# Expert stage of a two-layer decoder step: tokens split once, dispatch in float32r, the gate applied in the accumulate, the combine over five banks

## The chip, the cores and the metric

The program runs on one core of one Trainium2 chip. The metric is the device time of one execution in microseconds (us); lower is better. The engines are TensorE (PE in the rows; PEld is its weight load), VectorE (DVE), ScalarE (ACT), GpSimd (POOL) and SyncE (SP), which issues the loads of weights.

## The reference, cut to what matters

Two layers of a hybrid decoder are computed for 256 prompt tokens and 8 sample tokens, in float32. The change is in the last stage, the mixture of experts: each token goes to its two best experts of eight, with gates from a softmax over the two logits.

```
def moe_swiglu(h, router_w, wg, wu, wd):
    logits = (h @ router_w).astype(jnp.float32)
    top_v, top_i = lax.top_k(logits, TOP_K)
    gates = jax.nn.softmax(top_v, axis=-1)
    comb = jnp.sum(jax.nn.one_hot(top_i, N_EXPERTS, dtype=jnp.float32) * gates[..., None], axis=-2)
    out = jnp.zeros_like(h)
    for e in range(N_EXPERTS):
        out = out + comb[..., e:e + 1].astype(h.dtype) * swiglu(h, wg[e], wu[e], wd[e])
    return out
```

The model width is 1024 and an expert is 3584 wide, so an expert has three matrices of 1024 x 3584 (44.04 MB in float32).

## The kernel before, in words

Large products are made in three passes of float32r: each operand is split into a high part (ScalarE copies it to a float32r tile) and a low part (VectorE subtracts the high part from the original), and TensorE adds lo x hi, hi x lo and hi x hi in one PSUM bank. Weights come as pieces of 1 MB (128 partitions x 2048 floats). SyncE loads them into seven raw places (six in `weight_ring`, one in `work`); `take_hi` (L467 is its copy) and `take_lo` (L470 its subtraction) write the halves into three places of `weight_hi` and `weight_lo`. The dense layers in front do the same by L762 to L764.

An expert takes 42 pieces: seven steps c = 0..6, each with a gate product g, an up product u (both by `product`, L2009 to L2011: two pieces, 24 matmuls of 512 columns) and, one step late, a down product (`down`, L2024). Products go to banks 0 to 3 (g into bank 0 or 2, u into 1 or 3), transposes of the activation to bank 4 (L1993), the expert's output to banks 5 and 6.

Around the weights, per expert:

- `select` (DVE, L1534 and L1535) writes two matrices of one row per token and one column per slot (128 slots): `sel` with ones where the token's rank is the slot, and `selw` with the token's gate in that place. It runs for the next expert in step c = 2, behind the activation product L1557 and in front of the next L470.
- `dispatch` (PE, L1983) gathers the expert's tokens: `h_tok` (264 tokens in three tiles of 128, 128 and 8, float32) times `sel`, 24 matmuls of 128 columns into banks 7 and 3. It runs in front of the last `down`. L1048 (ACT) and L1542 (DVE) split the result into `hte_h` and `hte_l`, the second waiting for the first.
- Behind the g product of step 0 of the next expert comes `combine` (PE, L2040 and L2041) for the expert that is done: six tiles (two halves of 512 columns by three token tiles), two matmuls each, into the three banks 7, 3, 2 in turn. From the fourth tile on PE waits for `add_up` (DVE, L1584) to have emptied the bank of three tiles before. `add_up` stands in DVE's order behind `take_lo` of the fourth piece.
- Then PE transposes `sel` into bank 4 (L2058, three) and multiplies `selw` with a column of ones (L2060, three), which gives the gate of each slot. ACT copies that column to `slot_gate` (L1076) and the transposes to `ST` (L1077); `slot_gate` scales the output when it is split into `y_hi` (L1070) and `y_lo` (L1571).

The order within each engine is the program's; there is no scheduler. ACT and DVE follow PE through the counts `piece_used`, `hi_done` and `lo_done`. Before the first expert PE transposes x and h to token rows (L1962, 24 each through banks 0 to 3), ACT copies them (L1042), and masks and ranks are made in between (L1479 to L1522, L1968, L1972).

Of the kernel before, what the change touches and what calls it, by code (L numbers as in the profile page):

```python
# [14 lines left out]
P = 128  # L15
# [8 lines left out]
def program(nc, A, O):  # L24
# [31 lines left out]
    with ExitStack() as ctx:  # L56
# [30 lines left out]
        def order(engine, *events):  # L87
            first = 0
            for name, count in events:
# [11 lines left out]
              ("xtok", 6), ("htok", 6))  # L101
# [8 lines left out]
              ("iota_psum", 1), ("logits_psum", 1), ("xtok_psum", 6), ("htok_psum", 6), ("ranks_psum", 1))  # L110
# [7 lines left out]
              ("out_o_added", KD), ("norm3_inv", 1), ("norm3_done", 1), ("iota", 1), ("top_diff", 1), ("masks", 1), ("ranks", 1))  # L118


# [35 lines left out]
        W = 17696  # L156
        work = sb("work", [P, W])
# [248 lines left out]
        h_tok = cut(QKV0, NTT, D)  # L406
        raw_last = cut(QKV0 + NTT * D, PIECE)
        mo = [QKV0 + NTT * D + PIECE]

        def more_of(*dims):  # L410
            v = cut(mo[0], *dims)
            mo[0] += math.prod(dims)
            assert mo[0] <= W
            return v

        sel = more_of(NTT, CAP)
        selw = more_of(NTT, CAP)
        slot_gate = more_of(1)
# [13 lines left out]
        FAR = 16384.0  # L432

# [350 lines left out]
        def _(act_e):  # L784
# [253 lines left out]
            for s, dst in (("xtok", acc), ("htok", h_tok)):  # L1038
                for i, (t0, n) in enumerate(TOK):
                    for k in range(YC):  # L1040
                        act_e.wait_ge(*at(s + "_psum", i * YC + k + 1))
                        SC.activation(dst[0:n, i, k * CHUNK_COLS:(k + 1) * CHUNK_COLS],  # L1042
                                      bank[(i * YC + k) % 4][0:n, :], ACT.Copy).then_inc(sig(s), 1)

            def dispatch_out(it, r):
                act_e.wait_ge(*at("moe_disp", it * 2 + r + 1))
                n = KD // 2
                SC.activation(hte_h[:, r * n:(r + 1) * n, :], bank[(7, 3)[r]][:, :].rearrange("p (j t) -> p j t", j=n), ACT.Copy)\  # L1048
                  .then_inc(sig("hte_hi"), 1)
# [5 lines left out]
            def act_expert(it, more):  # L1055
                for n, (kind, c, part) in enumerate(order_e):
# [10 lines left out]
                    if n == PER - 1:  # L1067
                        wait_used(act_e, it, "d", NSTEP - 1)
                        for hf in range(YC):
                            SC.activation(y_hi[:, hf * CHUNK_COLS:(hf + 1) * CHUNK_COLS], bank[5 + hf][:, :], ACT.Copy,  # L1070
                                          scale=slot_gate).then_inc(sig("y_high"), 1)
# [24 lines left out]
        def _(dve):  # L1096
# [380 lines left out]
            norm_dve(dve, 3, "ln_ffn_o", link)  # L1477
            dve.wait_ge(*at("iota_psum", 1))
# [34 lines left out]
            last.then_inc(sig("masks"), 1)  # L1513
            dve.wait_ge(*at("ranks_psum", 1))
# [16 lines left out]
            def select(e):  # L1531

                for i, (t0, n) in enumerate(TOK):
                    V.tensor_scalar(sel[0:n, i, :], iota[0:n, 0:CAP], column(rank, i, n, e), None, ALU.is_equal)  # L1534
                    last = V.tensor_scalar(selw[0:n, i, :], iota[0:n, 0:CAP], column(rank, i, n, e), column(comb, i, n, e),  # L1535
                                           ALU.is_equal, ALU.mult)
                last.then_inc(sig("sel"), 1)

            def hte_lo(it, r):
                dve.wait_ge(*at("hte_hi", it * 2 + r + 1))  # L1540
                n = KD // 2
                V.tensor_tensor(hte_l[:, r * n:(r + 1) * n, :], bank[(7, 3)[r]][:, :].rearrange("p (j t) -> p j t", j=n),  # L1542
                                hte_h[:, r * n:(r + 1) * n, :].bitcast(F32), ALU.subtract).then_inc(sig("hte"), 1)
# [6 lines left out]
            def dve_expert(it, owed, more, e_next):  # L1550
                for n, (kind, c, part) in enumerate(order_e):
                    if kind == "g" and part and c:
                        tr_lo(it, c - 1)
                    if kind == "u" and part:
# [3 lines left out]
                        if c == 2 and more:  # L1558
                            dve.wait_ge(*at("moe_w", it + 1))
                            select(e_next)  # L1560
# [5 lines left out]
                    if n == PER - 1:  # L1566
                        wait_used(dve, it, "d", NSTEP - 1)
                        for hf in range(YC):
                            cols = slice(hf * CHUNK_COLS, (hf + 1) * CHUNK_COLS)
                            dve.wait_ge(*at("y_high", it * YC + hf + 1))  # L1570
                            V.scalar_tensor_tensor(y_lo[:, cols], bank[5 + hf][:, :], slot_gate, y_hi[:, cols].bitcast(F32),  # L1571
                                                   ALU.mult, ALU.subtract).then_inc(sig("y_out"), 1)
                    if n == 1 and owed:
                        add_up(it - 1)
# [3 lines left out]
            def add_up(it):  # L1578
                for k in range(NTT * YC):
# [4 lines left out]
                    V.tensor_tensor(a, a, bank[(7, 3, 2)[k % 3]][0:n, :], ALU.add).then_inc(sig("added"), 1)  # L1584
# [5 lines left out]
            dve_expert(0, False, True, 1)  # L1590
            with dve.Fori(1, NE - 1) as e:
                dve_expert(e, True, True, e + 1)
# [540 lines left out]
```

## Time and profile before

| what | value |
|---|---|
| median of 3 runs | 2059.72 us (2058.79 to 2063.31) |
| profiled execution, first to last instruction | 2062.8 us |
| PE busy | 1855.5 us, 90% of the span |
| DVE busy | 1366.5 us, 66% |
| ACT busy | 1041.4 us, 50% |
| mean granted clock of TensorE | 0.904 |
| expert stage | from about 955 us to the end |

The profile gives no other time of its execution than the span; it is 3.1 us above the median of the runs. "Busy" of PE counts pipelined matmuls as long as they last, so distances between starts say more than durations: a 512-column float32r matmul lasts 0.39 us and the next starts 0.23 us later.

### The profile page before, as it was taken

Reading aid. Unit: us, or ns where it says so; the run is one execution under the profiler, and the core shown is the slowest. Engines: PE = TensorE matmul, PEld = TensorE weight load, DVE = VectorE, ACT = ScalarE, POOL = GpSimd, SP = SyncE. Lnnn points to the kernel's source line nnn. Section 1 sums busy time; section 2 is a strip of 40 time slices with the busy share of each in tenths; the row PEclk is TensorE's granted clock in tenths of the full one; section 3 lists DMA queues with packets and bytes.
Section 4 is the critical chain, followed back from the end, with each engine's and each line's share of the span. In section 5 each row is a group of like instructions: output and inputs, shape, how many; then the busy total and the mean of one; then the engine's idle time right before and its main releaser. Section 6 shows DMA issues by size and latency. Waiting matters only on the chain.

```text
span 2062.8 us, 25677 instructions
## 1 busy us (share of the span) xinstructions
PE 1855.5 (90%) x9920; PEld 1566.0 (76%) x9920; DVE 1366.5 (66%) x1599; ACT 1041.4 (50%) x964; POOL 41.0 (2%) x92
## 2 busy tenths in 40 slices
PE   4967789998988678878999999999999999999997
PEld 4935689898976666476887887878878878788786
DVE  3564334444776555542887878878868788688786
ACT  3442233333652211022776766757757667577574
POOL 1011000000001000000000000000000000000000
PEclk9975789997998887575999999999999999999999
DMA  6443125442450002420897988988969889789794
GB/s 194 146 160 85 70 94 178 160 165 97 164 175 16 1 1 62 112 88 15 314 378 266 363 329 290 369 285 325 373 244 365 319 301 365 282 319 370 278 368 153
DMA packets 199084, 445.51 MB, mean 216 GB/s; under 512 B 9457, under 2 KB 20883, under 8 KB 198959
## 3 DMA queue, kind: packets, MB, share of 16 engines
q1 hardware_dynamic: 182206, 423.75, 57.1%
q0 software_dynamic: 3872, 12.85, 2.2%
q10 hardware_dynamic: 12924, 7.77, 1.3%
q8 instruction: 57, 0.93, 0.2%
q14 instruction: 25, 0.20, 0.0%
HBM read 437.28 MB, written 7.29 MB: 216 GB/s over the span
## 4 chain that ended last, share of the span: by engine, by line
PE 75%; DVE 11%; ACT 6%; issue 3%; PEld 2%; DMA 1%; ACTq 1%; PEldq 0%; DVEq 0%; POOLq 0%; POOL 0%
PE bank L2024 13%; PE bank L2009 10%; PE bank L2010 9%; PE bank L2011 9%; PE bank L762 5%; PE bank L763 5%; PE bank L764 4%; PE bank L1983 4%; ACT weight_hi L467 2%; DVE weight_lo L470 2%; PE bank L707 1%; PE bank L1861 1%; PE bank L1993 1%; PE bank L1856 1%; DVE work L1320 1%
## 5 line engine op out<-in xcount | busy, mean ns | idle before, releaser
L470 DVE TENSOR_TENSOR weight_lo<-weight_ring,weight_hi 128x2048 fp32r<-128x2048 f32 (+1 forms) x358 | 810.2, 2272 | 356.6 <-ACT weight_hi L467 356.5
L467 ACT ACTIVATE weight_hi<-weight_ring 128x2048 fp32r<-128x2048 f32 (+1 forms) x358 | 681.0, 1904 | 370.1 <-PE bank L764 152.3
L2009 PE MATMUL bank<-weight_hi,h_lo 128*128 128x512 f32 x896 | 360.4, 402 | 3.8 <-DVE weight_lo L470 2.3
L2010 PE MATMUL bank<-weight_lo,h_hi 128*128 128x512 f32 x896 | 353.7, 395 | 0.0
L2011 PE MATMUL bank<-weight_hi,h_hi 128*128 128x512 f32 x896 | 353.5, 395 | 0.0
L762 PE MATMUL bank<-h_hi,weight_lo 128*128 128x264 f32 x1072 | 313.7, 293 | 26.1 <-DVE h_lo L742 14.2
L763 PE MATMUL bank<-h_lo,weight_hi 128*128 128x264 f32 x1072 | 311.0, 290 | 0.0
L764 PE MATMUL bank<-h_hi,weight_hi 128*128 128x264 f32 x1072 | 309.0, 288 | 0.0
L762 PEld LDWEIGHTS bank<-h_hi,weight_lo 128*128 128x128 f32 x1072 | 208.2, 194 | 32.4 <-DVE h_lo L742 15.8
L763 PEld LDWEIGHTS bank<-h_lo,weight_hi 128*128 128x128 f32 x1072 | 208.2, 194 | 0.0
L764 PEld LDWEIGHTS bank<-h_hi,weight_hi 128*128 128x128 f32 x1072 | 207.6, 194 | 0.0
L2009 PEld LDWEIGHTS bank<-weight_hi,h_lo 128*128 128x128 f32 x896 | 171.4, 191 | 41.1 <-DVE weight_lo L470 4.5
L2011 PEld LDWEIGHTS bank<-weight_hi,h_hi 128*128 128x128 f32 x896 | 171.0, 191 | 36.9
L2010 PEld LDWEIGHTS bank<-weight_lo,h_hi 128*128 128x128 f32 x896 | 171.5, 191 | 34.2
L2024 PE MATMUL bank<-weight_hi,h_lo 128*128 128x512 f32 x448 | 139.3, 392 | 1.8 <-DVE h_lo L1547 1.8
L2024 PE MATMUL bank<-weight_lo,h_hi 128*128 128x512 f32 x448 | 138.8, 391 | 0.0
L2024 PE MATMUL bank<-weight_hi,h_hi 128*128 128x512 f32 x448 | 138.5, 390 | 0.0
L470 DVE TENSOR_TENSOR weight_lo<-work,weight_hi 128x2048 fp32r<-128x2048 f32 x48 | 109.9, 2290 | 12.7 <-ACT weight_hi L467 12.7
L467 ACT ACTIVATE weight_hi<-work 128x2048 fp32r<-128x2048 f32 x48 | 92.2, 1921 | 28.4 <-PE bank L2011 22.0
L2024 PEld LDWEIGHTS bank<-weight_hi,h_lo 128*128 128x128 f32 x448 | 83.8, 188 | 19.9 <-DVE h_lo L1547 2.1
L2024 PEld LDWEIGHTS bank<-weight_hi,h_hi 128*128 128x128 f32 x448 | 84.6, 189 | 17.8
L2024 PEld LDWEIGHTS bank<-weight_lo,h_hi 128*128 128x128 f32 x448 | 84.5, 189 | 17.6
(422 smaller groups left out, 1828.9 us busy)
## 6 DMA issues: line engine op xcount, KB each, us to landing
weight_ring<-in_moe_wg SPq DMA_DIRECT2D x104, 1024.0 KB, 6.8
weight_ring<-in_moe_wu SPq DMA_DIRECT2D x96, 1024.0 KB, 7.3
weight_ring<-in_moe_wd SPq DMA_DIRECT2D x88, 1024.0 KB, 6.2
work<-in_moe_wd SPq DMA_DIRECT2D x24, 1024.0 KB, 7.1
weight_ring<-in_w_in_o SPq DMA_DIRECT2D x8, 2048.0 KB, 8.5
work<-in_moe_wu SPq DMA_DIRECT2D x16, 1024.0 KB, 5.2
weight_ring<-in_w_in_e SPq DMA_DIRECT2D x5, 2048.0 KB, 14.0
weight_ring<-in_ffn_wg SPq DMA_DIRECT2D x5, 2048.0 KB, 7.9
```

Of the source, the lines that this page charges most:

```text
L467: return SC.activation(whi[:, p % SPLIT, 0:size], src, ACT.Copy).then_inc(sig("hi_done"), 1)
L470: V.tensor_tensor(wlo[:, p % SPLIT, 0:size], src, whi[:, p % SPLIT, 0:size].bitcast(F32), ALU.subtract)\
L707: last = PE.matmul(bank[4][0:m, i:i + 1], inv[:, j, t0:t0 + m], ones[:, 0:1], start=j == 0, stop=j == KD - 1)
L762: PE.matmul(out, lo[:, jj, cols_], h_hi[:, j0 + j, :], start=first and j == 0, stop=False)
L763: PE.matmul(out, hi[:, jj, cols_], h_lo[:, j0 + j, :], start=False, stop=False)
L764: last = PE.matmul(out, hi[:, jj, cols_], h_hi[:, j0 + j, :], start=False, stop=last_one and j == k - 1)
L1320: V.scalar_tensor_tensor(o[:, back:TP], x[:, 0:TP - back], tap(m, j), o[:, back:TP], ALU.mult, ALU.add)
L1983: last = PE.matmul(bank[(7, 3)[r]][:, jj * CAP:(jj + 1) * CAP], h_tok[0:n, i, j * P:(j + 1) * P], sel[0:n, i, :], start=i == 0, stop=i == ...
L2009: PE.matmul(out, hte_l[:, j, :], hi[:, jj, :], start=j == 0, stop=False)
L2010: PE.matmul(out, hte_h[:, j, :], lo[:, jj, :], start=False, stop=False)
L2011: last = PE.matmul(out, hte_h[:, j, :], hi[:, jj, :], start=False, stop=j == KD - 1)
L2024: last = PE.matmul(bank[5 + hf][:, :], lhs[:, c % 2, k, :], rhs[:, kk, hf * CHUNK_COLS:(hf + 1) * CHUNK_COLS], start=c == 0 and k == 0 and ...
```

## The change

- `h_tok` is split once into `tok_hi` and `tok_lo` (float32r, by the new ACT copy and DVE subtraction through six banks). The third token tile is padded with zeros to 128 rows, for which DVE writes three memsets.
- `dispatch` multiplies both parts with `sel`, which is float32r now, into a bank each: 48 matmuls in place of 24, and always 128 rows deep. ACT copies the high bank and DVE the low bank; neither waits for the other.
- `selw`, the products with the column of ones, `slot_gate` and its copy are gone. `add_up` multiplies by the token's gate as it adds.
- `combine` goes over five banks: 7, 3, 2, 5, 6. PE waits for `add_up` from the sixth tile on.
- Before the first expert, h is transposed first, then ranks, then x. `work` is placed first in SBUF, so that float32r tiles can lie over it.

```
-            for s, dst in (("xtok", acc), ("htok", h_tok)):
+            act_e.wait_ge(*at("tok_clear", 2))
+            for s, dst, banks in (("htok", tok_hi, TOK_BANKS), ("xtok", acc, X_BANKS)):
...
-            SC.activation(y_hi[...], bank[5 + hf][:, :], ACT.Copy, scale=slot_gate).then_inc(sig("y_high"), 1)
+            SC.activation(y_hi[...], bank[5 + hf][:, :], ACT.Copy).then_inc(sig("y_high"), 1)
...
-                        SC.activation(slot_gate, bank[4][:, T:T + 1], ACT.Copy)
...
+            V.memset(tok_hi[:, TT, :].bitcast(F32), 0.0).then_inc(sig("tok_clear"), 1)
+            V.memset(tok_lo[:, TT, :].bitcast(F32), 0.0).then_inc(sig("tok_clear"), 1)
+            V.memset(sel[:].bitcast(F32), 0.0).then_inc(sig("tok_clear"), 1)
...
+                    dve.wait_ge(*at("htok", i * YC + k + 1))
+                    V.tensor_tensor(tok_lo[0:n, i, part], bank[TOK_BANKS[i * YC + k]][0:n, :], tok_hi[0:n, i, part].bitcast(F32), ALU.subtract)\
+                     .then_inc(sig("htok_lo"), 1)
...
-                    V.tensor_scalar(sel[0:n, i, :], iota[0:n, 0:CAP], column(rank, i, n, e), None, ALU.is_equal)
-                    last = V.tensor_scalar(selw[0:n, i, :], iota[0:n, 0:CAP], column(rank, i, n, e), column(comb, i, n, e),
-                                           ALU.is_equal, ALU.mult)
+                    last = V.tensor_scalar(sel[0:n, i, :], iota[0:n, 0:CAP], column(rank, i, n, e), None, ALU.is_equal)
...
             def hte_lo(it, r):
-                dve.wait_ge(*at("hte_hi", it * 2 + r + 1))
+                dve.wait_ge(*at("moe_disp", it * 2 + r + 1))
...
-                    V.tensor_tensor(a, a, bank[(7, 3, 2)[k % 3]][0:n, :], ALU.add).then_inc(sig("added"), 1)
+                    V.scalar_tensor_tensor(a, bank[COMBINE_BANKS[k % 5]][0:n, :], column(comb, i, n, e), a, ALU.mult, ALU.add)\
+                     .then_inc(sig("added"), 1)
...
-                        last = PE.matmul(bank[(7, 3)[r]][:, jj * CAP:(jj + 1) * CAP], h_tok[0:n, i, j * P:(j + 1) * P],
-                                         sel[0:n, i, :], start=i == 0, stop=i == NTT - 1)
+                for part, src in enumerate((tok_hi, tok_lo)):
+                    for jj in range(KD // 2):
+                        j = r * (KD // 2) + jj
+                        for i in range(NTT):
+                            last = PE.matmul(bank[DISPATCH_BANKS[r][part]][:, jj * CAP:(jj + 1) * CAP], src[:, i, j * P:(j + 1) * P],
+                                             sel[:, i, :], start=i == 0, stop=i == NTT - 1)
...
-                    if k >= 3:
-                        pe.wait_ge(*at("added", (it + 1) * (NTT * YC) + (k - 2)))
+                    if k >= 5:
+                        pe.wait_ge(*at("added", (it + 1) * (NTT * YC) + (k - 4)))
...
-                        for i, (t0, n) in enumerate(TOK):
-                            last = PE.matmul(bank[4][:, T:T + 1], selw[0:n, i, :], ones[0:n, 0:1], start=i == 0, stop=i == NTT - 1)
```

## Rows read from the trace of the kernel before

**Rows 1.** The page: busy us (share of the span) and instructions of each engine.

```profile
PE 1855.5 (90%) x9920; PEld 1566.0 (76%) x9920; DVE 1366.5 (66%) x1599; ACT 1041.4 (50%) x964; POOL 41.0 (2%) x92
```

**Rows 2.** The page: the chain that ended last, by engine.

```profile
PE 75%; DVE 11%; ACT 6%; issue 3%; PEld 2%; DMA 1%; ACTq 1%; PEldq 0%; DVEq 0%; POOLq 0%; POOL 0%
```

**Rows 3.** The chain in order of time, end of one expert: start, us, what.

```profile
1223.70 0.44 PE bank L1993 x4
1224.14 8.24 PE bank L1983 x48
1232.38 5.68 PE bank L2024 x24
```

**Rows 4.** Timeline of PE, a dense layer: starts, durations, line and shape.

```profile
520.85 0.28 PE L764 MATMUL bank<-h_hi,weight_hi 128*128 128x264 f32 x1
...
522.05 0.29 PE L762 MATMUL bank<-h_hi,weight_lo 128*128 128x264 f32 x1
```

**Rows 5.** Timeline of PE, first dispatch; granted clock (PEclk) behind the busy times.

```profile
956.57 15.03 PE L1983 MATMUL bank<-work 128*128 128x128 f32 x48 [2.96 <-DVE work L1535]
973.01 0.79 PE L2009 MATMUL bank<-weight_hi,h_lo 128*128 128x512 f32 x1 [1.41 <-DVE h_lo L1542]
...
957.00:971.50 14.50, 14.50 (x48) 10.94 (x47) 0.69 (x1) 0.60 (x1) 0.00 (x0) 0.50 0.01 1
```

**Rows 6.** Timeline between two experts at 1238 us: DVE and ACT.

```profile
1239.53 1.40 DVE L1571 SCALAR_TENSOR_TENSOR h_lo<-bank,work,h_hi 128x512 fp32r<-128x512 f32 x2
...
1244.42 2.29 DVE L470 TENSOR_TENSOR weight_lo<-weight_ring,weight_hi 128x2048 fp32r<-128x2048 f32 x1 [0.94 <-ACT weight_hi L467]
1246.63 3.65 DVE L1584 TENSOR_TENSOR work<-work,bank 128x512 f32<-128x512 f32 x6
...
1241.18 1.28 ACT L467 ACT_TABLE_LOAD   x1
```

**Rows 7.** Timeline of PE, the combine between two experts at 1110 us.

```profile
1110.67 0.39 PE L2041 MATMUL bank<-h_hi,sel_slots 128*8 128x512 f32 x1
1113.58 0.50 PE L2040 MATMUL bank<-h_lo,sel_slots 128*128 128x512 f32 x1 [2.52 <-DVE work L1584]
...
1115.24 0.54 PE L2058 MATMUL bank<-ident,work 128*128 128x128 f32 x3
...
1116.55 0.50 PE L2009 MATMUL bank<-weight_hi,h_lo 128*128 128x512 f32 x1
```

**Rows 8.** Timeline in step c = 2: DVE, then PE.

```profile
1289.31 0.28 DVE L1534 TENSOR_SCALAR work<-work 128x128 f32<-128x128 f32 x1
...
1290.67 4.47 DVE L470 TENSOR_TENSOR weight_lo<-weight_ring,weight_hi 128x2048 fp32r<-128x2048 f32 x2
...
1293.00 0.50 PE L2009 MATMUL bank<-weight_hi,h_lo 128*128 128x512 f32 x1 [0.33 <-DVE weight_lo L470]
```

**Rows 9.** Windows over two boundaries: PE, PEld, DVE, ACT, POOL busy, clock, DMA share, GB/s.

```profile
1108.00:1122.00 14.00, 11.48 (x53) 8.44 (x52) 10.20 (x10) 8.65 (x8) 0.00 (x0) 1.00 0.75 256
1244.80:1258.80 14.00, 11.48 (x40) 8.64 (x40) 8.14 (x9) 5.66 (x6) 0.00 (x0) 0.76 0.65 224
```

**Rows 10.** Timeline of DVE: starts of the output's split, later experts.

```profile
1105.74 1.40 DVE L1571 SCALAR_TENSOR_TENSOR h_lo<-bank,work,h_hi 128x512 fp32r<-128x512 f32 x2
...
1376.32 1.40 DVE L1571 SCALAR_TENSOR_TENSOR h_lo<-bank,work,h_hi 128x512 fp32r<-128x512 f32 x2
...
1924.88 0.75 DVE L1571 SCALAR_TENSOR_TENSOR h_lo<-bank,work,h_hi 128x512 fp32r<-128x512 f32 x1
```

**Rows 11.** Timeline of PE: the other long waits of the stage.

```profile
1931.78 0.47 PE L2040 MATMUL bank<-h_lo,sel_slots 128*128 128x512 f32 x1 [1.58 <-DVE work L1584]
...
2043.44 0.72 PE L2024 MATMUL bank<-weight_hi,h_lo 128*128 128x512 f32 x2 [1.84 <-DVE h_lo L1547]
...
2052.42 0.50 PE L2040 MATMUL bank<-h_lo,sel_slots 128*128 128x512 f32 x1 [1.63 <-DVE h_lo L1571]
```

**Rows 12.** DMA from 1150 to 1838 us: rate in 40 slices.

```profile
GB/s 341 365 380 368 280 244 242 366 336 361 390 370 252 246 246 366 356 367 375 372 233 249 248 374 355 366 383 379 208 262 254 375 342 374 382 368 208 275 219 375
```

More of the change, by code:

```diff
@@ L117, in program, with over @@
               ("l2_applied", 2 * HC), ("s_prod", 1), ("on_inv", 1), ("on_applied", HC), ("on_done", 2), ("on_lo", 2),
-              ("out_o_added", KD), ("norm3_inv", 1), ("norm3_done", 1), ("iota", 1), ("top_diff", 1), ("masks", 1), ("ranks", 1))
+              ("out_o_added", KD), ("norm3_inv", 1), ("norm3_done", 1), ("iota", 1), ("top_diff", 1), ("masks", 1), ("htok_lo", 6), ("ranks", 1))
+        W = 17696
+        WORK_AT = -(-nc.sbuf_base // 32) * 32
+        work = sb("work", [P, W])
+        assert nc.sbuf_base == WORK_AT + 4 * W
+        def over(name, at_, shape, dt):
+            assert at_ + math.prod(shape[1:]) <= W
+            return nc.alloc_sbuf_tensor_at(name, shape, dt, offset=WORK_AT + 4 * at_)
         ring = sb("weight_ring", [P, SLOTS, KD * CHUNK_COLS])
@@ L1559, in dve_expert @@
                             dve.wait_ge(*at("moe_w", it + 1))
-                            select(e_next)
+                            select(e + 1)
                     if n == PER - 3:
@@ L1952, in _ @@
             last.then_inc(sig("logits_psum"), 1)
-            for s, src in (("xtok", xT), ("htok", hT)):
-                for i, (t0, n) in enumerate(TOK):
-                    for k in range(YC):
-                        r = i * YC + k
-                        if r >= 4:
-                            pe.wait_ge(*at(s, r - 3))
-                        elif s == "htok":
-                            pe.wait_ge(*at("xtok", NTT * YC))
-                        for m in range(KF):
-                            last = PE.transpose(bank[r % 4][0:n, m * P:(m + 1) * P], src[:, k * KF + m, t0:t0 + n], ident[:])
-                        last.then_inc(sig(s + "_psum"), 1)
+            pe.wait_ge(*at("iota", 1))
+            for i, (t0, n) in enumerate(TOK):
+                for k in range(YC):
+                    for m in range(KF):
+                        last = PE.transpose(bank[TOK_BANKS[i * YC + k]][0:n, m * P:(m + 1) * P], hT[:, k * KF + m, t0:t0 + n], ident[:])
+                    last.then_inc(sig("htok_psum"), 1)
             pe.wait_ge(*at("masks", 1))
@@ L1973, in _ @@
             last.then_inc(sig("ranks_psum"), 1)
-            pe.wait_ge(*at("htok", NTT * YC))
+            for i, (t0, n) in enumerate(TOK):
+                for k in range(YC):
+                    r = i * YC + k
+                    if r < 4:
+                        pe.wait_ge(*at("htok_lo", r + 1))
+                    else:
+                        pe.wait_ge(*at("xtok", r - 3))
+                    for m in range(KF):
+                        last = PE.transpose(bank[X_BANKS[r]][0:n, m * P:(m + 1) * P], xT[:, k * KF + m, t0:t0 + n], ident[:])
+                    last.then_inc(sig("xtok_psum"), 1)
+            pe.wait_ge(*at("htok_lo", NTT * YC))
+            pe.wait_ge(*at("xtok", NTT * YC))
             pe.wait_ge(*at("flag", 1))
@@ L2057, in pe_expert @@
                         for i, (t0, n) in enumerate(TOK):
-                            PE.transpose(bank[4][:, t0:t0 + n], sel[0:n, i, :], ident[0:n, 0:n])
-                        for i, (t0, n) in enumerate(TOK):
-                            last = PE.matmul(bank[4][:, T:T + 1], selw[0:n, i, :], ones[0:n, 0:1], start=i == 0, stop=i == NTT - 1)
+                            last = PE.transpose(bank[4][:, t0:t0 + n], sel[0:n, i, :].bitcast(F32), ident[0:n, 0:n])
                         last.then_inc(sig("moe_w"), 1)
```

64 lines of the change are left out of this document (33 added, 31 removed).

## The prediction

> **What bounds the kernel now.** I read the page first: TensorE is busy 90% of the span, VectorE 66%, ScalarE 50% [rows 1]. Then the chain of waits: PE carries 75% of it, DVE 11%, ACT 6% [rows 2]. So what PE does in the expert stage is on the path, and what DVE and ACT do is on it only where PE stands still. The chain in order of time shows the change's first piece: at the end of an expert the dispatch takes 8.24 us between the transposes and the last down product, and the down product runs on behind it without a gap [rows 3]. Last I read the timeline between two experts. PE runs the next g product and three combine tiles, then idles 2.52 us for the first `add_up` and does the rest [rows 7]; `add_up` starts at 1246.63, as soon as DVE is through the piece begun at 1244.42, which itself waited for ACT (a table load stands there) [rows 6]. In step c = 2 PE idles 0.33 us more, behind DVE [rows 8].
>
> I make the sum against the profiled execution, 2062.8 us from first to last instruction, and take off the 3.1 us by which it stands over the median of 2059.72.
>
> **The dispatch.** Before: 24 float32 matmuls, 48 records, 8.24 us [rows 3], so 0.172 us a record and 0.343 a matmul. After: 48 float32r matmuls of 128 moving columns. No float32r matmul under 264 columns is in the trace, so this price is unknown. From below: a float32 transpose, one record with 128 columns each way, costs 0.44 / 4 = 0.11 us [rows 3]. The float32r matmul of 264 columns costs (522.05 - 520.85) / 10 = 0.12 [rows 4]; a shorter one should not cost more. From above: the same as the float32 matmul of this shape, 0.343. I take 0.114, between the two single-record rows, since a float32r matmul is one record everywhere in this trace: 48 x 0.114 = 5.5 us, or 2.7 us less. Seven dispatches in the loop: 7 x 2.74 = 19.2 us (17 to 21 by the two near rows, a loss of 7 x 8.3 = 58 by the far one). The padded third tile costs nothing by itself: tiles of 8 rows already count in the 48 records like full ones. Behind the dispatch ACT's and DVE's copies start from its end as before, and so does ACT's first new piece; it all shifts with PE.
>
> The Trainium skill would price it lower (TensorE: Matmul & The Clock Gate, Back-to-back issue gap): a sustained stream of weight load and matmul at 128 columns takes about 81 ns a matmul. By that the dispatch would be an estimated 3.9 us and the loop's gain 30 us. The trace's one-record transposes, at 110 ns, don't run that fast, so I leave it out of the sum.
>
> The eighth, in front of the first expert, ran its 15.03 us at a granted clock of 0.50, the 1.2 GHz level [rows 5]. At twice 5.5 it takes 11.0: 4.0 us less. Behind it PE waited 1.41 us for ACT's copy and then DVE's [rows 5]; now they run side by side, which takes the shorter of the two, some 0.6 us, off. Its start I leave where it is. `select` has half the instructions (0.7 us less) and PE's h transposes no longer wait behind x. But DVE has six subtractions of 512 columns, 0.6 to 0.7 us each, between masks and ranks, and PE's x transposes end later. The three memsets lie under the router product, when DVE idles. Together 4.6 us, between 1 and 7.
>
> **The combine and the gate products.** DVE's order up to `add_up` is unchanged, so PE still waits for its first addition to end. Before, at the full clock, 2.97 us passed from then to the first matmul of the u product (1113.58 to 1116.55) [rows 7]: tiles four to six, three transposes, three products with the column of ones. After, only tile six is left, about 0.48 us, and the transposes, 0.46 (1115.24 to 1115.70): 0.95. So 2.0 us at each of seven boundaries, 14.1. Expert 0, which has no combine, loses its three gate products, 0.85. Together 15.0. Tiles four and five run earlier, in time in which PE idled, and the idle shrinks from 2.52 to about 1.6 us.
>
> What is late next: the fifth piece. `add_up` with a scalar per token costs what L1571 costs, 0.70 us apart [rows 6], where L1584 took 0.61; six of them end 0.5 us later, and PE comes to that piece 2 us earlier. By the rows it is ready some 0.6 us before PE needs it. If that cover is gone it costs up to 0.5 us a boundary, 3.5 in all. The last `add_up`, behind the last expert, is exposed: 0.1 to 0.5 us, within the rest.
>
> **The selection in step 2.** Six instructions in 1.36 us (1289.31 to 1290.67), then two pieces, then PE starts late [rows 8]. Three are left, 0.7 us less. PE's idle there is 0.33 us by the row; starts are about 0.7 us late against the usual 0.23 us distance. I take 0.65 x 7 = 4.6 us (2.3 if the row's idle is all).
>
> **The clock.** At one boundary of two shown the granted clock stays 1.00 over 14 us, at the other it is 0.76 [rows 9]; of the other four that the loop runs through, each falls too, and the one in front of the last expert doesn't. The price: from 1105.74 to 1239.53 are 133.8 us, from 1239.53 to 1376.32 (with 1239.53 in [rows 6]) 136.8 [rows 6, 10]. So a fall costs 3.0 us. From 1105.74 to 1924.88 six experts take 819.1 us [rows 10]; six times 133.8 is 802.7, so the five falls cost 16.4 (one is longer than the others). Which idle brings a fall? 2.52 us brought one at five of six boundaries. Of the other three long waits of the stage, 1.58 and 1.63 us brought none and 1.84 brought one [rows 11]. The idle of 1.6 us after the change lies with the first two, but it is followed by small work. I take two falls out of seven boundaries: 10.4 us gained (16.4 with none, a loss of 5 with seven).
>
> **The sum:** 19.2 + 4.6 + 15.0 + 4.6 + 10.4 = 53.8 us. 2062.8 - 53.8 = 2009.0 in the profile, 2006 as a median.
>
> **Rivals.**
>
> *A short float32r matmul is no cheaper than a float32 one* (the other side). At 0.343 us each, the dispatch takes 16.5 us: 11 more than in my sum, seven times, and 22 more in the first: 99 us, so 2105. For it: no row of the trace shows float32r at 128 columns, and float32 at that shape costs three times a transpose. Against: at 264 and 512 columns float32r costs one record a matmul. It decides from about 0.24 us a matmul on, where the dispatch's loss eats the other 30 us. The Trainium skill speaks against it (FP8 and Floating Point Precision): true float32 is four passes through the array. By it 48 single passes replace 96.
>
> *A short float32r matmul costs in between*, from the 0.172 us of a float32 record to 0.22. The dispatch is then 8.3 to 10.6 us; 25 to 46 us of the sum go: 2031 to 2052.
>
> *The clock goes on falling.* Everything else as forecast, but five to seven falls: 9 to 15 us more, 2015 to 2021. For it: the fall at 1.84 us is near, and after the wait come a tile of 8 tokens and transposes. Against: the fall-free waits of 1.58 and 1.63.
>
> *The loads become the bound.* An expert would have about 128 us for its 44.04 MB, 345 GB/s, and between boundaries already takes 366 to 384 [rows 12]. So the pace inside an expert is one the loads hold now, and no wait of ACT's copies for a load is seen. Only the pauses shrink, where the rate sinks to 210 to 280. If the loads could hold just 340 GB/s on average, it would cost some 2 us an expert: 2022.
>
> **Chances.** My forecast (dispatch at 0.08 to 0.14 us a matmul, up to four falls) 0.60; clock falling on 0.14; in between 0.15; loads 0.04; no cheaper 0.07. Less than 0.2%, 4 us, can't be told from no change by runs like these. All but the last rival end below 2055: faster 0.91; slower 0.07, and 0.02 for a price that hits the break-even. The likeliest case by itself spans 1990 (no fall, 0.08 us a matmul) to 2017. The range reaches to the in-between case's middle: 1990 to 2042.
>
> **What would show it.** L1983's successor: 48 records in about 5.5 us behind the transposes; 8 or more is a rival. PE's wait for `add_up` at 1.6 us, before the last tile alone. The u product 0.95 us after it. No idle before the g product of step 3. Granted clock near 1.00 at most boundaries. From one L1571 to the next about 128 to 129 us where the clock holds. The prediction is wrong if the short float32r matmuls are not single records, or if the earlier PE meets a piece of weights that is not yet split.

## The result, and the profile after

| kernel | median, us | lowest to highest | profiled span |
|---|---|---|---|
| before, in the same session | 2059.26 | 2057.53 to 2063.31 | 2062.8 |
| changed | 1990.7 | 1985.54 to 1993.12 | 1988.1 |

The ratio is 0.9657, 95% interval 0.9641 to 0.9672: 3.4% faster. On the 2059.72 us that the forecast started from this is 1989.1 us. The forecast was 2006, with a range from 1990 to 2042: the direction is right, and the gain of 70.6 us is larger than the 53.8 of the forecast, and just past the end of its range. The same kernel run again in a later session gave 1985.47 us (1984.19 to 1989.14), ratio 0.9641 (0.9623 to 0.966), so two sessions of one kernel lie up to 5 us apart.

The page of the changed kernel, busy times and the chain by engine. PE loses 59 us of busy time against [rows 1], and its share of the chain rises from 75% [rows 2] to 78%: less of the path is now time in which PE stands still.

```profile
PE 1796.3 (90%) x9872; PEld 1533.9 (77%) x9872; DVE 1368.7 (69%) x1584; ACT 1039.4 (52%) x956; POOL 41.0 (2%) x92
...
PE 78%; DVE 10%; ACT 4%; issue 2%; PEld 2%; DMA 1%; ACTq 1%; PEldq 0%; POOLq 0%; DVEq 0%; POOL 0%
```

The chain in order of time, at the end of one expert (start, us, what). This answers [rows 3]: the dispatch takes 5.31 us where it took 8.24.

```profile
1201.40 0.44 PE bank L2019 x4
1201.84 5.31 PE bank L2009 x48
1207.15 5.54 PE bank L2050 x24
```

The timeline of PE at the first dispatch, and two windows over it (us, busy of PE, PEld, DVE, ACT, POOL, granted clock, DMA share, GB/s). It answers [rows 5].

```profile
949.90 1.53 PE L2009 MATMUL bank<-sel,tok_hi 128*128 128x128 f32 x12 [0.72 <-issue]
...
955.29 2.76 PE L2009 MATMUL bank<-sel,tok_lo 128*128 128x128 f32 x12
958.88 0.76 PE L2035 MATMUL bank<-weight_hi,h_lo 128*128 128x512 f32 x1 [0.83 <-ACT h_hi L1060]
...
949.90:952.50 2.60, 2.60 (x23) 2.60 (x24) 0.00 (x0) 0.00 (x0) 0.00 (x0) 0.99 0.02 6
952.50:958.10 5.60, 5.55 (x27) 5.36 (x26) 0.70 (x2) 0.61 (x2) 0.00 (x0) 0.50 0.00 0
```

The 15.03 us have become 8.1 (949.90 to 958.05). The first half of the matmuls now runs at a granted clock of 0.99 (the 2.4 GHz level), the rest at 0.50 (1.2 GHz). In front PE waits 0.72 us, not 2.96, and behind 0.83, not 1.41.

The timeline of PE and DVE between two experts, answering [rows 7]. One combine tile, the last, is left behind the wait. From its start to the first u product 0.93 us pass.

```profile
1091.97 0.39 PE L2067 MATMUL bank<-h_hi,sel_slots 128*128 128x512 f32 x1
1093.05 4.02 DVE L1602 SCALAR_TENSOR_TENSOR work<-bank,work 128x512 f32<-128x512 f32 x6
1093.85 0.39 PE L2066 MATMUL bank<-h_lo,sel_slots 128*8 128x512 f32 x1 [1.50 <-DVE work L1602]
...
1094.32 0.54 PE L2085 MATMUL bank<-ident,sel 128*128 128x128 f32 x3
1094.78 0.50 PE L2035 MATMUL bank<-weight_hi,h_lo 128*128 128x512 f32 x1
```

Windows over two boundaries, same columns, answering [rows 9]. The granted clock is 1.00 at both, and so it is at the other five.

```profile
1086.00:1100.00 14.00, 12.51 (x57) 9.56 (x56) 12.35 (x13) 10.78 (x8) 0.00 (x0) 1.00 0.81 291
1214.00:1228.00 14.00, 12.51 (x57) 9.57 (x56) 12.36 (x13) 10.81 (x8) 0.00 (x0) 1.00 0.79 290
```

The timeline of DVE, start of the output's split, answering [rows 10]. From the first to the second row is one expert, 128.0 us; from the first to the third are six, 768.3 us, 128.05 each.

```profile
1086.14 1.28 DVE L1589 TENSOR_TENSOR h_lo<-bank,h_hi 128x512 fp32r<-128x512 f32 x2
...
1214.17 1.28 DVE L1589 TENSOR_TENSOR h_lo<-bank,h_hi 128x512 fp32r<-128x512 f32 x2
...
1854.45 1.28 DVE L1589 TENSOR_TENSOR h_lo<-bank,h_hi 128x512 fp32r<-128x512 f32 x2
```

From these marks, profile against profile, the 74.7 us divide so:

| stretch | forecast | measured |
|---|---|---|
| up to the router product (935.73 before, 930.01 after) | 0 | 5.7 |
| h/x transposes to the first split of an output (162.76, now 148.88) | 8.8 | 13.9 |
| six experts (819.14, now 768.31) | 42.8 | 50.8 |
| last expert and end (137.92, now 133.65) | 2.0 | 4.3 |

The rest is rounding. By this table alone the forecast looks right in kind and short in size. The experiments say otherwise of its first term.

### The profile page after: what moved, and what is told of

It reads as the page before. It is cut to its first block, busy times and chain, and to the rows that moved or that the text cites. A ratio compares the mean times of both kernels' runs of the same rounds, so it can differ in the third digit from the quotient of the medians.

```text
span 1988.1 us, 25554 instructions
## 1 busy us (share of the span) xinstructions
PE 1796.3 (90%) x9872; PEld 1533.9 (77%) x9872; DVE 1368.7 (69%) x1584; ACT 1039.4 (52%) x956; POOL 41.0 (2%) x92
## 4 chain that ended last, share of the span: by engine, by line
PE 78%; DVE 10%; ACT 4%; issue 2%; PEld 2%; DMA 1%; ACTq 1%; PEldq 0%; POOLq 0%; DVEq 0%; POOL 0%
PE bank L2050 15%; PE bank L2035 10%; PE bank L2037 10%; PE bank L2036 10%; PE bank L773 5%; PE bank L774 5%; PE bank L775 5%; PE bank L2009 2%; PE bank L718 1%; ACT weight_hi L478 1%; DVE weight_lo L481 1%; PE bank L1880 1%; PE bank L2019 1%; PE bank L1875 1%; DVE work L1331 1%
## 5 line engine op out<-in xcount | busy, mean ns | idle before, releaser
L2035 PE MATMUL bank<-weight_hi,h_lo 128*128 128x512 f32 x896 | 355.5, 397 | 0.8 <-ACT h_hi L1060 0.8
L2050 PE MATMUL bank<-weight_hi,h_lo 128*128 128x512 f32 x448 | 138.5, 390 | 1.8 <-DVE h_lo L1565 1.8
L2050 PE MATMUL bank<-weight_lo,h_hi 128*128 128x512 f32 x448 | 138.1, 389 | 0.0
```

The costliest lines, as they stand in the source:

```text
L2035: PE.matmul(out, hte_l[:, j, :], hi[:, jj, :], start=j == 0, stop=False)
L2050: last = PE.matmul(bank[5 + hf][:, :], lhs[:, c % 2, k, :], rhs[:, kk, hf * CHUNK_COLS:(hf + 1) * CHUNK_COLS], start=c == 0 and k == 0 and ...
```

## Experiments: what makes the dispatch shorter

**Float32 again in the changed kernel.** The dispatch goes back to one float32 operand, with the padding kept. ACT splits the high part and DVE subtracts behind it, as before the change.

```
-tok_hi = over("tok_hi", ..., F32R); sel = over("sel", ..., F32R)
+tok_hi = over("tok_hi", ..., F32);  sel = over("sel", ..., F32)
-for part, src in enumerate((tok_hi, tok_lo)):
+for part, src in enumerate((tok_hi,)):
```

> The changed kernel with its dispatch back in float32: 24 float32 matmuls over tokens and sel padded to 128 rows, split by ScalarE's copy and VectorE's subtraction one after the other; the subtractions for tok_lo still run, on zeros. Theory A, by the two profiles: a dispatch of 8.24 us in place of 5.31, seven times, 20.5 us; and the first one, at 0.17 us a record where the clock is full and 0.31 where it is half, 3 to 7 us more with its serial copies 0.7: 24 to 28 us over the changed kernel's 1991, so 2015 to 2019. Rival B, float32 matmuls let the clock fall behind the dispatch and float32r ones keep it up: falls come back between experts, 3 us each, 2030 or more.

Measured: 1987.34 us (1984.81 to 1991.59), ratio 0.964 (0.962 to 0.966). That is the changed kernel's time. The chain, and a window over the first dispatch:

```profile
1203.06 0.44 PE bank L2019 x4
1203.50 5.36 PE bank L2009 x48
...
955.30:961.00 5.70, 5.60 (x48) 5.41 (x48) 0.69 (x1) 0.66 (x2) 0.00 (x0) 1.00 0.01 3
```

48 float32 records take 5.36 us, 0.112 each, where the kernel before needs 8.24 for as many. The granted clock doesn't fall between its experts either. Both theories fell with this: float32r is neither what made the dispatch shorter nor what keeps the clock up. What stands out of what is left of the dispatch is the depth of the third token tile, 128 rows with zeros against 8. This kernel differs from the kernel before in the other parts of the change too, so the depth has to be tried by itself.

**The padding alone, in the kernel before.** Two memsets (and a wait of ACT for them), and all 128 rows in the dispatch:

```
+V.memset(h_tok[:, TT, :], 0.0); V.memset(sel[:], 0.0)
-PE.matmul(..., h_tok[0:n, i, ...], sel[0:n, i, :], ...)
+PE.matmul(..., h_tok[:, i, ...], sel[:, i, :], ...)
```

> The kernel before with one edit: h_tok and sel have zeros in the unused 120 rows of the third token tile, and the dispatch multiplies 128 rows deep in all three tiles, still in float32. Theory A, which the run with the float32 dispatch brought (48 records in 5.36 us once all tiles were 128 rows deep): the price of the old dispatch lies in its tile of 8 rows between tiles of 128, not in float32. Then each dispatch in the loop takes 5.4 us in place of 8.24, 20 us in all, the first one 4 to 5 us less, and the count of clock falls may change with the shorter period (each 1.5 to 3 us): about 2034, 2018 to 2040. Rival B, padding is worth nothing alone: 2059.

Measured: 2028.21 us (2027.1 to 2029.68), ratio 0.9845 (0.9826 to 0.9863). From the chain and the timeline of PE:

```profile
1214.39 5.36 PE bank L1986 x48
...
956.58 8.15 PE L1986 MATMUL bank<-work 128*128 128x128 f32 x48 [2.96 <-DVE work L1538]
```

Nothing but zeros in 120 rows is added, and the dispatch falls from 8.24 to 5.36 us, the first from 15.03 to 8.15. This small edit brings 31 us, where the whole change brings 69. The seven dispatches in the loop have 20.2 of them and the first has 6.9, which is partly the clock (it is back at 1.00 from 962 us on, against 979 in the kernel before). The other 4 were not taken apart; the clock still falls at five boundaries.

**The changed kernel without the padding.** Float32r in two parts, third tile of 8 rows:

```
-for i in range(NTT): PE.matmul(..., src[:, i, ...], sel[:, i, :], ...)
+for i, (t0, n) in enumerate(TOK): PE.matmul(..., src[0:n, i, ...], sel[0:n, i, :], ...)
```

> The changed kernel with one edit: the dispatch stays in float32r in two parts, but its third token tile is 8 rows deep again. Theory A, the tile of 8 rows costs by breaking the stream, whatever the type: 48 records in about 8.2 us again, 20 us over the changed kernel in the loop and 3 to 8 in the first dispatch: 2012 to 2020. Rival B, float32r matmuls keep their 0.11 us a record beside tiles of 8 rows: 1991, no change.

Measured: 2068.8 us (2067.21 to 2072.63), ratio 1.0043 (1.0029 to 1.0056). Slower than before the change; in the changed kernel the padding is worth 78 to 83 us (against 1990.7 and 1985.47). The direction was expected, at about a third of the size. The chain, then windows over one dispatch (columns as above):

```profile
1221.46 0.44 PE bank L2019 x4
1221.90 12.86 PE bank L2009 x48
...
1222.00:1226.50 4.50, 4.50 (x23) 3.51 (x22) 1.62 (x2) 0.53 (x1) 0.00 (x0) 1.00 1.01 368
1227.00:1234.50 7.50, 7.50 (x24) 5.74 (x23) 0.39 (x1) 0.30 (x1) 0.00 (x0) 0.50 0.30 117
```

At a granted clock of 1.00 its loads of 8 rows start at 1222.62, 1223.24 and 1223.86 us, so three records take 0.62 us, 0.207 each, against 0.111 in the changed kernel. By that the 48 would take 9.9 us. The other 2.9 come from the second window: the clock falls to 0.50 inside the dispatch, in each of the seven experts that have one, although the profile shows PE busy all of the time. It stays down for 10.2 to 17.1 us, mostly 13.65, so the work behind it is slowed too: the period is 138.1 to 139.5 us, 10 to 11.5 over the changed kernel's 128.05, of which 7.55 lie in the dispatch shown. The expectation had only the changes of depth, and not the clock. Why the clock falls there is open.

The weight loads show where the stream breaks. The rows are those of the dispatch's line in the experts from 1190 to 1850 us, with minimum, median and maximum in ns; the kernel before, the changed one, and this one.

```profile
L1983 PEld LDWEIGHTS bank<-work x240: 181/189/192, 1223.9 to 1779.1; 128*128 128x128 f32 x80, 8*128 8x128 f32 x40
```

```profile
L2009 PEld LDWEIGHTS bank<-sel,tok_hi x144: 190/192/192, 1201.6 to 1845.7; 128*128 128x128 f32 x144
```

```profile
L2009 PEld LDWEIGHTS bank<-sel,tok_hi x120: 181/206/333, 1221.6 to 1786.0; 128*128 128x128 f32 x80, 8*128 8x128 f32 x40
L2009 PE MATMUL bank<-sel,tok_hi x120: 272/369/476, 1221.7 to 1786.0; 128*128 128x128 f32 x80, 8*128 8x128 f32 x40
```

A load by itself is no longer in the kernel before (192 ns at most) than in the changed one. The timeline of PEld in the kernel before, over one group of six records, shows what is:

```profile
1225.98 0.52 PEld L1983 LDWEIGHTS bank<-work 128*128 128x128 f32 x4
1226.62 0.29 PEld L1983 LDWEIGHTS bank<-work 8*128 8x128 f32 x2
1227.04 0.30 PEld L1983 LDWEIGHTS bank<-work 128*128 128x128 f32 x2
```

Four loads of 128 rows overlap each other and take 0.52 us. Then PEld stands idle for 0.12 us, the two loads of 8 rows take 0.29, and it is idle for 0.13 again. Start to start a load comes 0.11 us after one of its own depth, two of 8 rows as well, and 0.31 after one of the other. So the cost is neither a dearer instruction nor the short tile as such, but the change of depth, in either direction. In the float32r run, at a granted clock of 1.00, the distances are 0.11 us between equal depths and 0.25 to 0.26 at a change. That also accounts for float32r being the dearer type without padding: a float32 matmul has two records of one depth, so a dispatch of 48 records has 8 short stretches, and a float32r one, with one record a matmul, has 16.

**A third tile of 32 rows.**

```
-for i in range(NTT): PE.matmul(..., src[:, i, ...], sel[:, i, :], ...)
+for i, n in enumerate((P, P, 32)): PE.matmul(..., src[0:n, i, ...], sel[0:n, i, :], ...)
```

> The changed kernel with one edit: the third token tile of the dispatch is 32 rows deep, not 128 and not 8. Theory A, any tile that does not use all 128 rows breaks the stream: as with 8 rows, about 2069. Rival B, what costs is a depth under one group of 32 rows: 1991.

Measured: 2069.06 us (2063.63 to 2073.39), ratio 1.0047 (1.0031 to 1.0062). From the chain:

```profile
1217.15 12.80 PE bank L2009 x48
```

32 rows behave as 8 do, as the first theory had it. Depths between 32 and 128 were not tried.

## Experiments: the boundary between two experts and the clock

**The combine on three banks,** in the changed kernel:

```
-if k >= 5: pe.wait_ge(*at("added", ... + (k - 4)))     # bank k % 5
+if k >= 3: pe.wait_ge(*at("added", ... + (k - 2)))     # bank k % 3
```

> The changed kernel with its combine back on three banks, PE waiting from the fourth tile on. Theory A, a fall of the clock follows the length of PE's idle stretch: the idle is 2.5 us again, tiles four and five stand behind it (1.2 us at seven boundaries, 8 us), and falls of 3 us come back at most of seven boundaries, 12 to 21 us: 2011 to 2020. Rival B, the falls of before came with the small products with the column of ones or the float32 dispatch: no falls, 8 us more, 1999.

Measured: 2000.39 us (1997.65 to 2002.03), ratio 0.9707 (0.9687 to 0.9728). The timeline of PE at one boundary, and windows over two:

```profile
1220.14 0.79 PE L2066 MATMUL bank<-h_lo,sel_slots 128*128 128x512 f32 x1 [2.40 <-DVE work L1602]
...
1083.00:1097.00 14.00, 11.60 (x50) 8.32 (x49) 12.10 (x12) 9.69 (x8) 0.00 (x0) 1.00 0.80 290
1212.40:1226.40 14.00, 11.60 (x46) 8.25 (x45) 12.30 (x12) 8.75 (x7) 0.00 (x0) 0.88 0.81 287
```

The idle is back at 2.4 us, close to the 2.52 of [rows 7]. An expert without a fall takes 129.3 us, 1.27 more. But of the six boundaries with this wait (at the seventh it is 1.46) the clock falls at only two, for 3.4 us each, where the kernel before had falls at five of its first six. The time is the one of the theory without falls, 1999, though there were two; the other theory, falls at most boundaries, is refuted.

**The gate products back,** in the changed kernel: `selw`, the three products with the column of ones, `slot_gate` and its copy, a plain add in `add_up`.

```
+last = V.tensor_scalar(selw[0:n, i, :], ..., ALU.is_equal, ALU.mult)
+last = PE.matmul(bank[4][:, T:T + 1], selw[0:n, i, :], ones[0:n, 0:1], ...)
-V.scalar_tensor_tensor(a, bank[...], column(comb, i, n, e), a, ALU.mult, ALU.add)
+V.tensor_tensor(a, a, bank[...], ALU.add)
```

> The changed kernel with the gate back in the output's split: selw, its three products with the column of ones, slot_gate and its copy, and add_up without the gate. Theory A: 0.85 us of PE in eight experts (6.8) and PE's late start in step 2 in seven (0.7 each, 4.6), the clock staying up since the idle is unchanged: 11 us more, 2002. Rival B, VectorE was not late in step 2, what went there was something else: 7 us, 1998. Rival C, the small products bring falls back: 2011 or more.

Measured: 2003.06 us (1997.84 to 2007.46), ratio 0.9719 (0.9696 to 0.9743). An expert without a fall takes 129.63 us, 1.59 more. The products have 0.85 of it, and the combine comes 0.12 later behind the start of the output's split (8.30 us to the transposes, against 8.18). The 0.62 that remain are those of step 2, where PE again waits for DVE. Windows over its first two boundaries:

```profile
1086.00:1100.00 14.00, 12.38 (x45) 9.50 (x44) 10.36 (x9) 7.38 (x8) 0.00 (x0) 0.76 0.75 261
1218.00:1232.00 14.00, 12.39 (x51) 9.55 (x50) 10.93 (x10) 8.76 (x9) 0.00 (x0) 0.88 0.78 269
```

The clock falls at both, though PE's idle there is 1.62 and 1.61 us, near the changed kernel's 1.50, which brings none. At the boundaries behind them the same idle of 1.61 us brings no fall. The time is near the 2002 of the first theory, which had the clock staying up; about 4.7 us of it are the two falls.

**Five banks alone,** in the kernel before, with only the order of the banks and the wait changed.

```
-if k >= 3: pe.wait_ge(*at("added", ... + (k - 2)))     # bank (7, 3, 2)[k % 3]
+if k >= 5: pe.wait_ge(*at("added", ... + (k - 4)))     # bank (7, 3, 2, 5, 6)[k % 5]
```

> The kernel before with one edit: the combine goes over the five banks 7, 3, 2, 5, 6, PE waiting from the sixth tile on. Theory A: tiles four and five run in the idle, 1.2 us at each of seven boundaries, 8 to 9 us less, as undoing it in the changed kernel cost 10; the five falls of the clock may stay or go, since the run with three banks showed that their number is not set by the idle stretch alone: 2050 with all, 2035 with none. Rival B, worth nothing alone: 2058.

Measured: 2044.72 us (2042.04 to 2046.93), ratio 0.9928 (0.9911 to 0.9944). An expert takes 132.57 us without a fall (133.8 before), 134.15 with one; the clock falls at three boundaries, for 3.4 us each; the idle is 1.61 or 1.62 us at each of the first six, with a fall or without. So the banks give 1.2 us an expert, here as in the other direction, some 9 of the 14 us; the rest is the clock: fewer falls, and shorter ones.

## Experiments: the work ahead of the first expert

**`work` placed first in SBUF,** alone in the kernel before; the change needs this, and router products start 5.7 us earlier in its profile.

```
+work = sb("work", [P, W])
 ring = sb("weight_ring", [P, SLOTS, KD * CHUNK_COLS])
...
-work = sb("work", [P, W])
```

> The kernel before with one edit: the tile work is placed first in SBUF, as the changed kernel has it. The changed kernel's profile reached the router product 5.7 us earlier than the profile of before (930.0 against 935.7 us), though nothing of the change runs ahead of it. Theory A, scatter from run to run (the clock's phase and the first loads): no difference, within 3 us of 2059. Rival B, the place of work in SBUF makes the dense stages faster: 5 to 6 us less, 2054, and a router product that starts at about 930 us.

Measured: 2057.71 us (2052.68 to 2063.21), ratio 0.9988 (0.9974 to 1.0001). At most 0.26%, and the router product starts at 935.8 us, as in the kernel before. The placement is not what brings the 5.7 us.

**x transposed first again,** in the changed kernel, with the order of ACT's and DVE's copies to match.

```
-order: h transposes, ranks, x transposes
+order: x transposes, h transposes, ranks
```

> The changed kernel with one edit: x is transposed before h, as in the kernel before, so that PE waits for ranks and selection with nothing to do. Theory A, the first stretch gained (the profiles: 13.9 us from the h or x transposes to the first split of an output, against 6 forecast) because x's transposes now fill that wait, the first dispatch starts sooner and the clock does not fall in front of it: 6 to 9 us more than the changed kernel, 1997 to 2000. Rival B, the padded dispatch alone brought it: 1991 to 1993.

Measured: 1993.16 us (1991.61 to 1999.74), ratio 0.9682 (0.9662 to 0.9703), 7.7 us over the changed kernel run beside it. The timeline of PE, and a window over the first dispatch:

```profile
944.35 5.16 PE L1979 MATMUL bank<-ident,xT 128*128 128x128 f32 x24
...
956.89 2.79 PE L2008 MATMUL bank<-sel,tok_hi 128*128 128x128 f32 x12 [2.14 <-DVE sel L1554]
...
957.00:967.00 10.00, 10.00 (x48) 10.00 (x48) 0.69 (x1) 0.60 (x1) 0.00 (x0) 0.50 0.01 2
```

From the transposes to the first output's split are 151.5 us, against 148.9: 2.6 us. The dispatch waits 2.14 us for `sel`, and all of it runs at a granted clock of 0.50. The profiled executions are 10.6 us apart (1997.8 and 1987.2), and 7.9 of them lie ahead of the edit: the router product starts at 937.1 us in this profile and at 929.2 in its neighbour's. Neither theory fits. The time is the second one's, but the changed kernel beside it is faster still, and the two intervals don't overlap; and the dispatch doesn't start later than with h first: 12.54 us behind the first transpose, against 12.64 in the changed kernel. Of the 2.6 us, 2.3 are the dispatch itself, 10.47 us against 8.15, and that is the granted clock. This clock changes with the same code: in the run below with the first addition ahead, whose order here is the changed kernel's, the first dispatch ran at 1.00 from end to end.

```profile
951.40:956.80 5.40, 5.38 (x48) 5.40 (x48) 0.69 (x1) 0.60 (x1) 0.00 (x0) 1.00 0.01 3
```

**The changed kernel again,** beside the two above, unedited:

> The changed kernel once more, unedited, as the measure for the others: 1991, and in its profile no fall of the clock between experts, one at most. If the stage before it scatters, its router product starts between 930 and 936 us.

Measured: 1985.47 us (1984.19 to 1989.14), span 1987.2, periods of 128.01 to 128.09 us, and again no fall between experts.

## Experiments: what is left at the boundary

With five banks PE still waits once, because `add_up` comes behind the fourth piece on DVE. Two versions of the changed kernel move it.

**The first addition ahead of the fourth piece:**

```
+if n == 0 and owed: add_up(it - 1, e - 1, range(0, 1))
-if n == 1 and owed: add_up(it - 1, e - 1)
+if n == 1 and owed: add_up(it - 1, e - 1, range(1, NTT * YC))
```

> The changed kernel, a try for a faster one: VectorE adds the first combine tile in front of the fourth piece of weights (in the 0.94 us in which it waits for ScalarE there) and the other five behind it as before. Theory A, PE's 1.5 us of idle before the sixth tile goes, and the fifth piece is ready in time: 1.5 to 1.9 us at each of seven boundaries, 11 to 13 us less than 1991: 1979. Rival B, the piece that PE needs next is then late by part of it, since VectorE is the one behind: half, 1985. Rival C, it only moves the idle to that piece: 1990.

Measured: 1980.45 us (1979.39 to 1987.47), ratio 0.9626 (0.9604 to 0.9648), period 127.0 us, 1.05 less than the changed kernel's: the 1979 of the first theory.

**The additions spread over three pieces:** one, two and three of them, and PE's wait for the last three moved from the g product of step 1 to its down product.

```
+if n == 0 and owed: add_up(it - 1, e - 1, range(0, 1))
+if n == 1 and owed: add_up(it - 1, e - 1, range(1, 3))
+if n == 2 and owed: add_up(it - 1, e - 1, range(3, NTT * YC))
```

> As the run with the first tile ahead, but the other tiles are spread as well: two behind the fourth piece, three behind the fifth, and PE waits for all six only before the first down product. If theory A of that run holds, this gives the same, 1979; if its rival B or C holds (the fifth piece late behind five additions), this one gets back what that one loses, 1979 against 1985 or 1990.

Measured: 1976.19 us (1975.07 to 1985.78), ratio 0.9607 (0.9583 to 0.963), period 126.5 us. The timelines of PE, then of DVE, at one boundary:

```profile
1213.71 0.39 PE L2071 MATMUL bank<-h_hi,sel_slots 128*128 128x512 f32 x1
1213.93 0.39 PE L2070 MATMUL bank<-h_lo,sel_slots 128*8 128x512 f32 x1
1214.16 0.39 PE L2071 MATMUL bank<-h_hi,sel_slots 128*8 128x512 f32 x1
1214.39 0.54 PE L2089 MATMUL bank<-ident,sel 128*128 128x128 f32 x3
...
1212.44 0.75 DVE L1606 SCALAR_TENSOR_TENSOR work<-bank,work 128x512 f32<-128x512 f32 x1 [0.80 <-PE bank L2071]
1215.31 1.39 DVE L1606 SCALAR_TENSOR_TENSOR work<-bank,work 128x512 f32<-128x512 f32 x2
1218.83 2.05 DVE L1606 SCALAR_TENSOR_TENSOR work<-bank,work 128x512 f32<-128x512 f32 x3
```

PE's starts are 0.22 to 0.23 us apart through the combine: the wait is gone. This is the shortest time of all that were run: 0.5 to 0.7% under the changed kernel's two medians, and 3.9% under the kernel before. The steadier sign is the period, 126.49 to 126.56 us in all six, against 128.0 to 128.1.

## Why the prediction was right, and where it was wrong

The direction was right, and the sum was 21 us too small against the profile. The clock between the experts gave 6.0 us more than its term, the first stretch 5.1, the last expert 2.3, the loop's dispatches and boundaries 2, and 5.7 lie ahead of the router product, where the sum has nothing. And behind one term whose size held, the dispatch, the mechanism was wrong.

**The dispatch.** Forecast 5.5 us, measured 5.31: the number held, and the reason did not. The step that failed is this one: "The padded third tile costs nothing by itself: tiles of 8 rows already count in the 48 records like full ones." It costs nothing indeed, but it is the gain itself. That the number held is luck: with float32r and no padding the same step measures 12.86 us. I read 0.172 us a record as the price of float32, and it was the mean of a stream in which full and short tiles alternate, 0.112 between equal tiles of 128 rows and about 0.2 around each change of depth. The four corners:

| dispatch | third tile of 8 rows | padded to 128 |
|---|---|---|
| float32, rest as before | 8.24 us, 2059 us in all | 5.36 us, 2028 |
| float32, rest changed | not run | 5.36 us, 1987 |
| float32r, rest changed | 12.86 us, 2069 | 5.31 us, 1985 to 1991 |

In the padded column the type makes no difference: a float32r record of 128 columns costs what a float32 record does (0.111 and 0.112 us), and two parts need as many records as one float32 operand. What I took from below, the transpose at 0.11 us, was the right row, and it was a float32 row of full depth: it could have told me that float32 isn't what costs 0.172. A float32r matmul is half as long as a float32 one, and there are twice as many.

**The first dispatch.** Forecast 11.0 us and 0.6 off the wait behind it; measured 8.1 and 0.58. The granted clock was 0.99 for its first half. Of the 5.1 us that this stretch gained beyond the forecast, 2.9 are the dispatch. Another 0.95 are its start, which I had left where it is: it came 13.59 us behind the first transpose before and 12.64 after. The order of the transposes is not the reason, since with x first it is 12.54. About 1.1 more are the products behind it, which run at 0.50 for 3.8 us, against 6.1. So most of it is the clock, and that is luck: the changed kernel's own code gave a dispatch of 8.1 us in two profiles, and variants with the same code up to there gave 5.4 us at 1.00 in three.

**The boundary.** Forecast 2.0 us at each and an idle of 1.6; measured 2.17 (the start of the output's split to the first u product: 10.81, now 8.64) and 1.50. The fifth piece was covered, as forecast. Undoing the parts gave 1.27 for the banks and 0.85 for the products, 2.12 together.

**Step 2.** Forecast 0.65 us an expert. 133.8 - 128.05 = 5.74; less 2.93 for the dispatch and 2.17 for the boundary, 0.64 remain, and undoing it cost 0.62.

**The clock.** This is the term that was mis-sized most: two falls forecast, none came, 16.4 us in place of 10.4. Shown is that there were none, in two sessions. The argument behind it, from the length of the idle, is refuted: 2.4 us brought a fall at two boundaries of six, and 1.61 us brought one at the second boundary of a kernel and none at its third. The kernel before with `work` moved has its five falls at other boundaries than the kernel before. What decides is open. Across the kernels the falls grow fewer as the loop has fewer and shorter pauses, but no run isolates that. The last expert has 2.3 us more than forecast. Some 1.6 of them are the fall behind the 1.84 us wait [rows 11], which is absent as well: the same wait is 1.83 us after, without one. The price of 1.6 is read from the run with the padding alone, whose last expert has no fall ahead of its output's split and takes 125.12 us to it, where the kernel before takes 126.74.

**Ahead of the change,** 5.7 us that no step of mine has. The router product started at 935.6 to 935.8 us in all four profiles of kernels with the old order, and anywhere from 929.2 to 937.1 in ten of the changed one and its variants, with nothing edited up to there but the placement, which by itself brings none of it. The cause stays open, and no run takes this stretch apart. Of the difference between forecast and profile, 21 us, this is a quarter.

**The rivals.** "The clock goes on falling" and "in between" did not come. "The loads become the bound" neither: an expert took 126.5 us in the last version, 44.04 MB / 126.5 = 348 GB/s, with no wait on a load.

**The range.** Its lower end, 1990, was meant as no fall and 0.08 us a matmul. By the sum's own terms that case is lower. At 0.08 each of seven dispatches is 1.6 us shorter and the first 3.3, and two falls more are saved for 6.0: 20.7 us under 2006, or 1985. The other end, four falls and 0.14, comes to about 2023, not 2017. So the likeliest case as described holds the 1989.1 that was measured, and the stated range doesn't.

## What to carry to other kernels

Before a price per instruction is carried over, split its group by shape: the mean of [rows 3] mixed two depths, and the whole dearness lay in the changes between them. Where tiles of unequal depth follow each other in a stream of short matmuls, pad the short one with zeros and measure that alone, before any change of type. An edit that does several things should be tried with each taken away; here the padding, made only for the sake of the float32r dispatch, carried nearly half of the gain.

## What the runs showed of the hardware

- In a stream of 128-column matmuls, one tile of 8 or of 32 rows among tiles of 128 costs more than one of 128: 2.88 us over eight short tiles in float32, 0.36 each, and at a granted clock of 1.00 in float32r 0.62 us for a group of three records against 0.33. The time goes at each change of depth: a load starts 0.31 us after one of another depth in float32 and 0.25 to 0.26 in float32r, and 0.11 after one of its own, also between two of 8 rows. The Trainium skill (TensorE: Matmul & The Clock Gate, Step-by-step: what each phase is for) says that a weight load's timing goes by its columns and that its row count doesn't matter. For a load by itself the trace agrees (181 to 192 ns in the kernel before); for the distance between loads it doesn't. The same page of the Trainium skill (The mechanism) has a load pulled ahead of running matmuls where its row groups don't conflict, or where it goes to the background weights. After a change of depth a load starts 0.20 us behind the start of the matmul before it in the kernel before, and within 0.11 us between equal depths. That a load isn't pulled ahead there would fit this, but no run here shows the reason.
- A float32 matmul of 128 columns is two records of 0.112 us, twice a float32r one of 0.111. The Trainium skill (FP8 and Floating Point Precision) gives four passes for true float32; the trace shows twice the time of float32r, not four times.
- The granted clock can fall to 0.50 while the profile shows PE busy without a gap: in each unpadded float32r dispatch of the loop, for 10.2 to 17.1 us. Idle of the same length, 1.61 us, brought a fall at some boundaries and none at others of one kernel, in two kernels.
